# A fourth Strassen pair, eight weight slots, and low parts added by DMA in a float32 decoder layer

## The reference

```
a = rmsnorm(h); z = a @ w_in                      # 2048 x 5120
o = concat(dilated_attention(q, k, v), conformer_conv(cv, cg))
h = h + o @ w_out                                 # 2048 x 2048
f = rmsnorm(h)
h = h + (silu(f @ w_gate) * (f @ w_up)) @ w_down  # 2048 x 5632 twice, 5632 x 2048
gte = sigmoid(rmsnorm(h) @ w_pgate + b_pgate)     # 2048 x 2048
h = h + (p @ w_ple) * gte
out = rmsnorm(h)
```

## Time and profile before

| | |
|---|---|
| median of 3 runs | 1170.06 us (1169.43 to 1171.83) |
| the profiled execution | 1169.63 us, of it 1167.8 us from the first to the last instruction (the span) |
| granted clock of TensorE, mean | 0.997 of 2.4 GHz |
| the loop's pass, between its transposes | 64.1 us, ten of them |
| DMA | 223.33 MB, mean 191 GB/s |

### The profile page before, as it was taken

One profiled execution on the slowest core, in us unless ns is written; L12 is line 12 of the kernel. 1 busy time (PEld: TensorE's weight loads), 2 busy tenths in 40 slices (PEclk: granted clock), 3 DMA queues, 4 the chain that ended last, 5 costly groups with the idle time before them and its releaser, 6 DMA issues.

```text
span 1167.8 us, 16352 instructions
## 1 busy us (share of the span) xinstructions
PE 1154.0 (99%) x5648; PEld 975.7 (84%) x5648; DVE 904.3 (77%) x1215; ACT 616.5 (53%) x790; POOL 137.4 (12%) x86
## 2 busy tenths in 40 slices
PE   9999999999999999999999999999999999999996
PEld 8889989988888788888888888888888888888886
DVE  6489767767777988887878787888878787857674
ACT  6544465466465654645555454546354554547552
POOL 0222443436024100000000000000000000000111
PEclk9999999999999999999999999999999999999998
DMA  9655555454654565564646564655646464484541
GB/s 344 211 180 181 180 181 169 159 179 145 213 168 163 186 243 180 195 214 166 224 167 224 174 218 156 239 178 198 216 161 230 165 228 168 147 304 163 195 165 72
DMA packets 113116, 223.33 MB, mean 191 GB/s; under 512 B 5193, under 2 KB 6417, under 8 KB 112816
## 3 DMA queue, kind: packets, MB, share of 16 engines
q1 hardware_dynamic: 112608, 222.08, 56.3%
q10 hardware_dynamic: 464, 0.66, 0.2%
HBM read 220.63 MB, written 2.10 MB: 191 GB/s over the span
## 4 chain that ended last, share of the span: by engine, by line
PE 91%; DVE 3%; issue 2%; ACT 2%; POOL 1%; DMA 1%; SPq 0%; DVEq 0%; POOLq 0%; ACTq 0%
PE ps L1408 13%; PE ps L1410 13%; PE ps L1409 13%; PE ps L1611 12%; PE ps L1613 12%; PE ps L1612 12%; PE ps L1442 3%; PE ps L1441 3%; PE ps L1440 3%; PE ps L1450 1%; DMA arena<-in_p 1%; DVE w_lo L955 1%; ACT w_hi L664 1%; PE ps L1606 1%; PE ps L1604 1%
## 5 line engine op out<-in xcount | busy, mean ns | idle before, releaser
L664 ACT ACTIVATE w_hi<-w_raw 128x1024 fp32r<-128x1024 f32 x306 | 324.0, 1060 | 357.3 <-PE ps L1410 180.0
L955 DVE TENSOR_TENSOR w_lo<-w_raw,w_hi 128x1024 fp32r<-128x1024 f32 x270 | 339.2, 1261 | 210.7 <-ACT w_hi L664 208.9
L1611 PE MATMUL ps<-w_hi,nT_hi 128*128 128x512 f32 x350 | 137.1, 392 | 0.0
L1613 PE MATMUL ps<-w_hi,nT_lo 128*128 128x512 f32 x350 | 136.3, 389 | 0.0
L1612 PE MATMUL ps<-w_lo,nT_hi 128*128 128x512 f32 x350 | 136.2, 389 | 0.0
L1408 PE MATMUL ps<-w_hi,oT_hi 128*128 128x512 f32 x320 | 125.8, 393 | 0.0
L1410 PE MATMUL ps<-w_hi,oT_lo 128*128 128x512 f32 x320 | 124.6, 390 | 0.0
L1409 PE MATMUL ps<-w_lo,oT_hi 128*128 128x512 f32 x320 | 124.5, 389 | 0.0
L1408 PE MATMUL ps<-w_hi,nT_hi 128*128 128x512 f32 x280 | 111.4, 398 | 0.0
L1410 PE MATMUL ps<-w_hi,nT_lo 128*128 128x512 f32 x280 | 109.1, 390 | 0.0
L1409 PE MATMUL ps<-w_lo,nT_hi 128*128 128x512 f32 x280 | 109.0, 389 | 0.0
(11 more groups left out here) (240 smaller groups left out, 2283.6 us busy)
## 6 DMA issues: line engine op xcount, KB each, us to landing
w_raw<-in_w_gate SPq DMA_DIRECT2D x88, 512.0 KB, 3.9
w_raw<-in_w_up SPq DMA_DIRECT2D x88, 512.0 KB, 4.7
w_raw<-in_w_down SPq DMA_DIRECT2D x44, 1024.0 KB, 5.0
w_raw<-in_w_in SPq DMA_DIRECT2D x32, 1024.0 KB, 5.1
w_raw<-in_w_out SPq DMA_DIRECT2D x16, 1024.0 KB, 5.0
w_raw<-in_w_pgate SPq DMA_DIRECT2D x16, 1024.0 KB, 5.0
w_raw<-in_w_in SPq DMA_DIRECT2D x14, 512.0 KB, 9.6
w_raw<-in_w_ple SPq DMA_DIRECT2D x2, 1024.0 KB, 5.9
```

The costliest lines, as they stand in the source:

```text
L664: nc.scalar.activation(tiles_of(m)[0], source_of(m), ACT.Copy).then_inc(hi_ready, 1)
L955: nc.vector.tensor_tensor(lo, source_of(m), hi.bitcast(F32), ALU.subtract).then_inc(lo_ready, 1)
L1611: nc.tensor.matmul(bank[:, :], x[0], w[0], start=first, stop=False)
L1613: return nc.tensor.matmul(bank[:, :], x[1], w[0], start=False, stop=last)
```

## The change

- The pattern of the chunk pairs becomes `PPSSPSSP`: four S and four P pairs. A pass has 24 + 8 = 32 units and 4 x 24 + 4 x 21 + 96 = 276 matmuls. GpSimd, ScalarE and VectorE make a fourth set of token sums before the loop.
- The low parts of the down units of columns 1 and 3 (four units a pass) aren't made by VectorE. ScalarE writes the negated high part into the low slot (L686 of the changed kernel), and a DMA that GpSimd issues adds the raw weights to it (L647). TensorE, and SyncE for the reload, wait for `lo_by_dma` of that column, for both its units.
- On every engine the first pass is written out ahead of the hardware loop, which now has eight passes. The first activation's low and high parts (`act_hi`, `act_lo`) stand before the splits of the seventh slot.
- Before the loop, the first activation (`swish_of`, `first_swiglu`) is called at unit `LOOP0 - 1`, ahead of that step's splits, instead of after all of them.
- `SMALL_AT` goes from 10 to 12.

```diff
-SMALL_AT, RB_AT = 10, 15
+SMALL_AT, RB_AT = 12, 15
-QUAD_KINDS = "PPSPSPSP"
+QUAD_KINDS = "PPSSPSSP"
-LOOP_SLOTS = 6
+LOOP_SLOTS = 8
+DMA_COLUMNS = (1, 3)
...
+def by_dma(m):
+
+    return in_loop(m) and loop_unit(m)[0] == "D" and loop_unit(m)[1] in DMA_COLUMNS
...
-    return sum(by_pool(i) == by_pool(m) for i in range(m + 1)) + PER_LOOP * it
+    return sum(by_pool(i) == by_pool(m) and not by_dma(i) for i in range(m + 1)) + (PER_LOOP - 2 * len(DMA_COLUMNS)) * it
...
+        w_extra = sb("w_extra", [P, 2, 4, NP], F32R)
...
-                    return tuple(o[:, 10:14].rearrange("p (k a) t -> p k (a t)", k=2) for o in (oT_hi, oT_lo))
+                    return tuple(o[:, 12:16].rearrange("p (k a) t -> p k (a t)", k=2) for o in (oT_hi, oT_lo))
                 if n == 5:
                     return w_more[:, 0:2], w_more[:, 2:4]
+                if n >= 6:
+                    return w_extra[:, n - 6, 0:2], w_extra[:, n - 6, 2:4]
...
             def down_split(c, it):
+                if c in DMA_COLUMNS:
+                    sp.wait_ge(lo_by_dma[c], 32 + 32 * it)
+                    return
...
+            done = 0
+            for m in filter(by_dma, range(LOOP0, PLE0)):
+                done += 1
+                pool.wait_ge(minus_hi_ready, done)
+                nc.gpsimd.dma_start(slot_of(m)[1], source_of(m), accum_op=ALU.add).then_inc(lo_by_dma[loop_unit(m)[1]], 16)
...
                 nc.scalar.activation(tiles_of(m)[0], source_of(m), ACT.Copy).then_inc(hi_ready, 1)
+                if by_dma(m):
+                    nc.scalar.activation(tiles_of(m)[1], source_of(m), ACT.Copy, scale=-1.0).then_inc(minus_hi_ready, 1)
...
             for m in range(IN0, LOOP0):
                 step(m)
+                if m == LOOP0 - 1:
+                    sc.wait_ge(rstd_ready, 3)
+                    swish_of(LOOP0)
...
-            sc.wait_ge(rstd_ready, 3)
-            swish_of(LOOP0)
             for m in range(LOOP0 + SLOTS, LOOP0 + LOOP_SLOTS):
+                if m == LOOP0 + SLOTS + 2:
+                    act_hi(ACT_BANKS, 0)
                 split_hi(m)
...
-                    if t == 2:
+                    if t == 2 and not first:
                         act_hi(ACT_BANKS, it)
...
+            feed_forward(0, False, True)
+            with sc.Fori(1, LOOPS - 1) as it:
...
+                if m == LOOP0 - 1:
+                    ve.wait_ge(panel_read, Q_DOWN)
+                    first_swiglu()
+                    split_lo(m + AHEAD)
...
-                if not by_pool(m + AHEAD):
+                if not by_pool(m + AHEAD) and m < LOOP0 - 1:
                     split_lo(m + AHEAD)
-            ve.wait_ge(panel_read, Q_DOWN)
-            first_swiglu()
...
             def arrived(m, it=0):
 
+                if by_dma(m):
+                    pe.wait_ge(lo_by_dma[loop_unit(m)[1]], 32 + 32 * it)
+                    return
...
-    nc = bacc.Bacc("TRN2", target_bir_lowering=False, num_devices=1)
+    nc = bacc.Bacc("TRN2", target_bir_lowering=False, num_devices=1, dynamic_dma_scratch_size=2048)
```

More of the change, by code:

```diff
@@ L371, in hybrid_decoder_layer @@
         w_sum_ready = sem("w_sum_ready")
+        minus_hi_ready = sem("minus_hi_ready")
+        lo_by_dma = {c: sem(f"lo_by_dma{c}") for c in DMA_COLUMNS}
         x_joined, x_normal, s_step, s_hi_ready, s_ready = sem("x_joined"), sem("x_normal"), sem("s_step"), sem("s_hi_ready"), sem("s_ready")
@@ L508, in feed_forward @@
                         load_quad(i, bass.ds(it * NP + 2 * NP, NP))
-            with sp.Fori(0, LOOPS - 1) as it:
+            feed_forward(0, False)
+            with sp.Fori(1, LOOPS - 1) as it:
                 feed_forward(it, False)
@@ L873, in _, with feed_forward @@
                 split_hi(m + AHEAD)
-            sc.wait_ge(rstd_ready, 3)
-            swish_of(LOOP0)
             for m in range(LOOP0 + SLOTS, LOOP0 + LOOP_SLOTS):
+                if m == LOOP0 + SLOTS + 2:
+                    act_hi(ACT_BANKS, 0)
                 split_hi(m)
-            def feed_forward(it, last):
+            def feed_forward(it, last, first=False):
                 for t in range(PER_LOOP):
-                    if t == 2:
+                    if t == 2 and not first:
                         act_hi(ACT_BANKS, it)
@@ L898, in feed_forward @@
                         split_hi(PLE0 + t + LOOP_SLOTS - PER_LOOP)
-            with sc.Fori(0, LOOPS - 1) as it:
+            feed_forward(0, False, True)
+            with sc.Fori(1, LOOPS - 1) as it:
                 feed_forward(it, False)
@@ L1246, in _, with feed_forward @@
                         weight_sums(m - LOOP0 - ahead, 0, i)
-                if not by_pool(m + AHEAD):
+                if not by_pool(m + AHEAD) and m < LOOP0 - 1:
                     split_lo(m + AHEAD)
-            ve.wait_ge(panel_read, Q_DOWN)
-            first_swiglu()
             for m in range(LOOP0 + SLOTS, LOOP0 + LOOP_SLOTS):
+                if m == LOOP0 + SLOTS + 2:
+                    act_lo(ACT_BANKS, 0)
                 split_lo(m)
-            def feed_forward(it, last):
+            def feed_forward(it, last, first=False):
                 for t in range(PER_LOOP):
-                    if t == 2:
+                    if t == 2 and not first:
                         act_lo(ACT_BANKS, it)
@@ L1294, in feed_forward @@
                 add_down(3, it)
-            with ve.Fori(0, LOOPS - 1) as it:
+            feed_forward(0, False, True)
+            with ve.Fori(1, LOOPS - 1) as it:
                 feed_forward(it, False)
@@ L1720, in feed_forward @@
                         tokens_by_columns(LOOP0 + DOWN_AT + 2 * c + k, DOWN_BANKS[c], oT_hi[:, rows], oT_lo[:, rows], k == 0, k == 1, it)
-            with pe.Fori(0, LOOPS - 1) as it:
+            feed_forward(0)
+            with pe.Fori(1, LOOPS - 1) as it:
                 feed_forward(it)
```

## The result

The changed kernel takes 1205.57 us (median of 4 runs, 1202.44 to 1209.4) where the kernel before takes 1169.83 us beside it: ratio 1.0296, 95% interval 1.0282 to 1.031. It is 36 us slower; 9 us faster was forecast. The profiled execution took 1209.4 us, of it 1207.6 us span.

What follows compares the result with a forecast made beforehand. TensorE's matmuls were taken to bound each pass. Gains of 6.80 (matmuls), 0.71 (p) and 1.3 us (loop entry) sum to 8.8 us, giving 1161 us; range 1157 to 1175, likeliest case 1158.5 to 1163.5.

Steps and rivals of the forecast that it cites:

- The 30 matmuls: Loop: a fourth Strassen pair removes 3 matmuls from each of 10 passes, 6.80 us, all on TensorE's path.
- VectorE's and ScalarE's totals: Per pass of 63.5 us: VectorE works 52.6 us, ScalarE 39.1 us; neither binds on average.
- the Strassen block: Two adjacent Strassen pairs: VectorE has about 12.9 us of work in TensorE's 9.5; counted nothing, up to 3.4 us a pass.
- The gap at 38 us: Before the loop, TensorE waits for p; moving its turn two units later gains 0.71 us, lower bound 0.
- one gap of 1.3 us: Loop entry: TensorE's 2.61 us gap becomes 1.3 us in the second unit; gain 1.3 us, bounds 0 and 2.6.
- the paragraph on SyncE behind the adding DMAs: Next pass's pair 1 reloads after column 1's adds: done 12.5, loaded 17.5, split due 18.3 us; cost nothing.
- a DMA share of 0.58: Loop pass: 2 MB more payload beside 12.6 MB was said to have room at this share.
- a slack of 0.8 us: Pair 1's load: loaded at about 17.5 us, split due at 18.3; other loads have 5 us or more.
- half a microsecond to one a pass: Price of splits finding no data when weights come late: 5 to 10 us in all, giving 1166 to 1171 us.
- The adds come late: Rival: at 7.8 us per add, one after the other, TensorE stands 3.5 us a pass; 1196 us; chance 0.20, either way.
- Its other way: GpSimd can't write DMA descriptors through VectorE's runs; pair late by about 3 us, near 1190 us; within the 0.20.
- The weights come late: Rival: adds crowd the loads, or SyncE's wait passes it on; 1166 to 1171 us; chance 0.14.

Runs made afterwards that it cites:

- the last kernels: Changed kernel with `w_extra` at a multiple of 64 bytes, fourth token-sum set two units later; no adds: 1162.72 us, column 3's adds only: 1161.15 us.

## Why the prediction was wrong

**Right.** The 30 matmuls are worth 0.68 us a pass, as the last kernels' 63.47 us against 64.15 show. VectorE's and ScalarE's totals hold, and VectorE fills the Strassen block with all low parts on top (56.9 us a pass without adds), although its work there was added up too low: by the durations quoted, two pairs of 6.93 us make 13.9 us and not 12.9. The gap at 38 us is gone.

**Nearly right.** At the entry one gap of 1.3 us was forecast; the changed kernel has two:

```profile
388.79 0.47 PE L1647 MATMUL ps<-w_hi,nT_hi 128*128 128x512 f32 x1 [0.34 <-DVE w_lo L983]
...
392.87 0.50 PE L1647 MATMUL ps<-w_hi,nT_hi 128*128 128x512 f32 x1 [1.11 <-DVE w_lo L983]
395.74 1.03 PE L1486 MATMUL ps<-ident,arena 128*128 128x128 f32 x8
```

The 1.11 us are the forecast one. For the other, the prediction took 389.1 us, the time of the kernel before, as the time at which TensorE wants unit 0's low part; with the 0.71 us gained at the start it wants it at 388.3. The first transposes come 1.46 us earlier than in the earlier trace rows, where 0.71 + 1.3 us were counted. What follows them was not worked out: the first pass is longer than the others even without adds (65.7 us), with a wait of 1.4 us for `h`.

**The step that failed** is the paragraph on SyncE behind the adding DMAs: "Adds done at 12.5, loaded at about 17.5 us; its split is due at 18.3. Nothing." On the same scale (ScalarE's first high part at 561.15 us stands for its 1.36) the negated parts came at 3.4 and 5.3 us, as worked out; the second add landed at 15.0 instead of 12.5 and the load at 22.7 instead of 17.5. Two sizes were off. The adds were taken at 6 us and take 8.8; the load was taken as one in a quiet loop, but ran beside column 3's adds, in a stretch with this row:

```profile
575.00:580.00 5.00, 5.00 (x24) 4.14 (x23) 3.84 (x6) 1.58 (x2) 0.00 (x0) 1.00 1.04 254
```

The argument that a DMA share of 0.58 has room was an average over the pass; in these 5 us the share is 1.04. Together 5.2 us late, against a slack of 0.8 us that the text had worked out and then counted as enough. And the price of missing it was put at half a microsecond to one a pass, since the list behind VectorE's waiting split was not read. It held the addition on which TensorE waits, and after six of nine such waits the clock fell too: 2.3 to 6.0 us a pass, 3.7 in the mean. That a late reload is not enough by itself, and column 3's adds are needed beside it, no part of the prediction had.

**The rivals.** "The adds come late" gives 1196 us, close to the time, but by a wait of TensorE for column 1, which happened once (2.1 us): in the pass shown column 1's matmuls start at 575.41 us, its adds landed at 574.75. Its other way, that GpSimd itself is late with its DMAs, does occur (in three of ten passes, by some 2 us), and nothing here shows that VectorE is the reason. "The weights come late" was the right mechanism, "SyncE's wait passes it on", with a price of 5 to 10 us, of which only the delay and not what stood behind it was counted.

**Not foreseen.** The address of `w_extra`, 5.5 us in all. Without adds, the expected gain of 8.8 us is so cut to about 1: 8.3 us of matmuls and start, less 5.5 us for the address and 1.4 to 1.7 us for the first pass.

In the profiled executions the changed kernel's span is 40.9 us longer than the one without adds: 4.8 us in the first pass (70.50 against 65.73), 29.7 in the next eight, 6.4 in the tenth and behind it. The first pass was not taken apart; TensorE stands in it 1.10 us for ScalarE's copy of a product, 2.08 us for column 1's adds and 0.82 us for `h`.

**Open.** Why an adding DMA takes longer and crowds more than a copy was not taken apart, nor why GpSimd issues some of them late, nor whether loads issued from another queue would fare better. A fifth raw buffer, which would free pair 1's reload from the adds, was not tried.

## What to carry to other kernels

When an engine's work is handed to a DMA, the DMA also becomes the last reader of its source: ask when that buffer is reloaded, and add the load behind it to the chain. Price a late datum by what is queued behind the instruction that waits for it, not by its own lateness, and a transfer by the share of the DMA engines in its own few microseconds, not by that of the pass. A slack smaller than the uncertainty of the terms that it is left over from is no slack.

## What the runs showed of the hardware

- An adding DMA of 512 KB within SBUF from GpSimd lands in 7.1 to 9.0 us (medians) beside the loop's loads, a plain copy in 6.9 us. With 40 adds that nobody waits for the up weights take 10.1 us, with 40 copies 5.7, and without either 4.7.
- Issuing such an add takes GpSimd 0.88 us, a plain copy of the same size 0.55 us.
- Matmuls of 512 columns whose moving operand starts 32 bytes past a multiple of 64 start every 0.2335 us, at a multiple of 64 every 0.2270 us.
- In the changed kernel, an idle time of 2.11 us within a pass is followed by eight starts 0.42 us apart, the 1.2 GHz level, and so are those of 1.80 and 1.82 us. Behind 2.84, 2.03 and 2.00 us there is no fall, nor behind the 1.11 us at the entry, where the next twelve matmuls take 2.87 us (392.87 to 395.74).
